# A decoder step: the multiply of LayerNorm's affine part moves from VectorE to GpSimd

## The reference, cut to what matters

```
x = layer_norm(ALPHA * x + gate * f(x), g, b)

def layer_norm(x, g, b):
    mu = mean(x); var = mean((x - mu)**2)
    return (x - mu) * rsqrt(var + 1e-5) * g + b
```

## Time and profile before

| | us |
|---|---|
| timed runs | 2422.81 median of 3 (2417.99 to 2425.23) |
| profiled execution, its own time | 2418.94 |
| its span, first to last instruction | 2417.2 |
| VectorE busy | 915.0 (38%), 1456 instructions |
| GpSimd busy | 388.4 (16%), 279 instructions |
| TensorE busy | 1675.2 (69%) |

### The profile page before, as it was taken

One profiled execution on the slowest core, in us unless ns is written; L12 is line 12 of the kernel. 1 busy time (PEld: TensorE's weight loads), 2 busy tenths in 40 slices (PEclk: granted clock), 3 DMA queues, 4 the chain that ended last, 5 costly groups with the idle time before them and its releaser, 6 DMA issues. The chain is left out here.

```text
span 2417.2 us, 21915 instructions
## 1 busy us (share of the span) xinstructions
PE 1675.2 (69%) x6774; PEld 695.2 (29%) x6775; DVE 915.0 (38%) x1456; ACT 387.5 (16%) x748; POOL 388.4 (16%) x279
## 2 busy tenths in 40 slices
PE   4565999487648999808977255555664739998980
PEld 1113444333323333304433122222221323333330
DVE  0112011547430000162020999999974450000006
ACT  0000011301112112221011111111111111221222
POOL 0000000000100000040020555555530100000004
PEclk8886999768759999958989566777777959999995
DMA  8884211142259989824220678778773066999973
GB/s 337 346 307 152 70 35 35 70 149 90 70 227 424 399 359 424 340 98 132 71 105 33 229 287 287 287 291 293 293 265 139 2 244 253 374 425 428 428 338 110
DMA packets 116715, 558.69 MB, mean 231 GB/s; under 512 B 13206, under 2 KB 22167, under 8 KB 101796
## 3 DMA queue, kind: packets, MB, share of 16 engines
q1 hardware_dynamic: 103000, 508.87, 54.3%
q0 software_dynamic: 7904, 28.45, 3.2%
q10 hardware_dynamic: 5740, 20.47, 2.1%
HBM read 517.62 MB, written 40.13 MB: 231 GB/s over the span
## 5 line engine op out<-in xcount | busy, mean ns | idle before, releaser
L1382 PE MATMUL ps<-arena_w,arena_r 128*64 128x512 f32 x1664 | 379.1, 612 | 31.3 <-issue 26.3
L1382 PEld LDWEIGHTS ps<-arena_w,arena_r 128*64 128x64 f32 x1664 | 126.9, 142 | 277.1 <-issue 270.9
L1364 PE MATMUL ps<-arena_w,arena_r 128*64 128x512 f32 x832 | 190.1, 605 | 19.2 <-ACT arena_r L1412 19.2
L1459 DVE TENSOR_TENSOR arena_r<-arena_r,ps 128x512 f32<-128x512 f32 x38 | 26.1, 688 | 439.9 <-ACT arena_r L1429 439.9
L1924 PE MATMUL ps<-arena_w,arena_r 128*32 128x512 f32 x504 | 146.0, 814 | 29.2 <-DMA arena_w<-in_cache_v_dram 29.2
L1878 POOL TENSOR_TENSOR xt<-arena_w,xt 128x1024 f32<-128x1024 f32 x48 | 121.1, 2523 | 161.7 <-DVE arena_w L2092 80.4
L352 PE MATMUL ps<-ident,arena_r 128*128 128x128 f32 (+1 forms) x200 | 41.8, 372 | 141.7 <-DVE arena_r L343 141.7
L151 PE MATMUL ps<-arena_w,arena_r 128*32 128x512 f32 x448 | 74.1, 823 | 58.2 <-DMA arena_w<-in_w_ada_dram 51.1
L1579 PE MATMUL ps<-arena_w,xt 128*128 128x512 f32 x256 | 111.8, 597 | 0.0
L441 PE MATMUL ps<-arena_w,xt 128*128 128x512 f32 x256 | 111.7, 597 | 0.0
L916 PE MATMUL ps<-arena_w,xt 128*128 128x512 f32 x256 | 111.1, 593 | 0.0
(11 more groups left out here) (315 smaller groups left out, 2282.7 us busy)
## 6 DMA issues: line engine op xcount, KB each, us to landing
arena_w<-in_w_exp_gate_dram SPq DMA_DIRECT2D x38, 2048.0 KB, 13.8
arena_w<-in_w_exp_up_dram SPq DMA_DIRECT2D x38, 2048.0 KB, 19.0
arena_w<-in_w_exp_down_dram SPq DMA_DIRECT2D x38, 2048.0 KB, 18.2
arena_w<-in_cache_v_dram SPq DMA_DIRECT2D x126, 512.0 KB, 5.2
arena_w<-in_w_ada_dram SPq DMA_DIRECT2D x12, 4096.0 KB, 13.4
arena_w<-in_cache_k_dram SPq DMA_DIRECT2D x96, 512.0 KB, 5.4
y_rows<-arena_r ACTq DMA_DIRECT2D x38, 512.0 KB, 10.7
lnr<-in_cache_k_dram SPq DMA_DIRECT2D x32, 512.0 KB, 5.8
```

Of the source, the lines that this page charges most:

```text
L1364: last = nc.tensor.matmul(psy[c][at:at + 64, :], ht[u][:, k, 64 * (1 - a):64 * (2 - a)], wd[u][:, k, c * 512:(c + 1) * 512], start=(k == 0 ...
L1382: last = nc.tensor.matmul(ps[at:at + 64, :], xgt[u][:, k, 64 * a:64 * (a + 1)], w[u][:, k, :], start=(k == 0), stop=(k == KT - 1), tile_po ...
```

## The change

`shift` is gone, with its five calls per stage. `offset`, which GpSimd runs, waits for `scaled` instead, does the product, signals `gained`, waits for that, and does the sum. The order of GpSimd's list is otherwise the same.

```diff
@@ stage_mix_output, VectorE
                 ln.mixed(v, i, r, [m.ps[b] for b in banks]).then_inc(ev, 1)
                 ln.stats(v, i, r)
-                if n:
-                    ln.shift(v, *order[n - 1])
-            ln.shift(v, *order[-1])
@@ LayerNorm
-    def shift(self, v, i, r):
-
-        nc, m = self.nc, self.m
-        self.scales += 1
-        v.wait_ge(self.scaled, self.scales)
-        nc.vector.tensor_tensor(m.x[0:r, i, :], m.x[0:r, i, :], m.lnr[0:r, 0, :], ALU.mult).then_inc(self.gained, 1)
-
     def offset(self, g, i, r):
         nc, m = self.nc, self.m
         self.offsets += 1
+        g.wait_ge(self.scaled, self.offsets)
+        nc.gpsimd.tensor_tensor(m.x[0:r, i, :], m.x[0:r, i, :], m.lnr[0:r, 0, :], ALU.mult).then_inc(self.gained, 1)
         g.wait_ge(self.gained, self.offsets)
         nc.gpsimd.tensor_tensor(m.x[0:r, i, :], m.x[0:r, i, :], m.lnr[0:r, 1, :], ALU.add).then_inc(self.done, 1)
@@ stage_combine, VectorE
                 ln.mixed(v, i, r, [y1[:, 0:512], y1[:, 512:1024]]).then_inc(f_ok, 1)
                 ln.stats(v, i, r)
-                if i:
-                    ln.shift(v, *TILES[i - 1])
-            ln.shift(v, *TILES[-1])
```

More of the change, by code:

```diff
@@ L944, in __init__ @@
         self.gained, self.done = sem("gained"), sem("done")
-        self.tiles = self.sds = self.scales = self.offsets = 0
+        self.tiles = self.sds = self.offsets = 0
     def mixed(self, v, i, r, halves):
```

## The result

| | before | changed |
|---|---|---|
| timed runs, median (lowest to highest) | 2422.25 us (2414.95 to 2426.34), 13 runs | 2430.87 us (2424.8 to 2436.11), 13 runs |
| ratio to before, 95% interval | | 1.0038 [1.0025, 1.005] |
| span of the profiled execution | 2417.2 us | 2429.1 us |
| combine stages, first gather's sum (L1496) to last add | 47.83, 47.83 us | 53.72, 53.70 us |
| output projections, last L952 to the next stage's L340 | 12.42, 12.41 us | 11.47, 11.46 us |

The ratio is +6 to +12 us, about a value of 9. The stages give 5.89 + 5.87 - 2 x 0.95 = +9.9 us. The two profiled spans differ by 11.9; the remaining 2 us lie in stretches in which both kernels run the same instructions, and such stretches vary from profile to profile.

The account below looks back on a forecast made before the run. VectorE's own sequence was taken to bound the combine stages, TensorE the output projections. Two combine stages at +6.5 us (+13.0) and projections at -1.9 gave +11.1 us, forecast 2432 us from a 2421.2 mean, range 2420 to 2438.

Parts of the forecast that it names:

- multiply 0: Combine stage: GpSimd's first multiply, behind tile 3's gathers, makes tile 2's weighted sum L1496 wait, +2.2 us.
- multiply 1: Combine stage: GpSimd's second multiply, behind tile 4's gathers, delays VectorE the same way again, +2.2 us.
- multiply 2 and add 2: Combine stage, tile 3: the multiply goes between the two L952, the add between the second and L960, +4.2 us.
- tile 4 to its last L971: Combine stage: multiply 3 and add 3 precede the second L952 and L960, 4.2 where one add cost 2.0, +2.2 us.
- behind it: Combine stage's end after the last L971: 6.3 us instead of 7.2, -0.9 us.
- end of a projection: After an output projection's last scaling: 4.8 us instead of 5.8, -0.94 us each, -1.9 for two.
- Strict turns: VectorE and GpSimd alternate whole instructions when both ask: combine stages +6.5 us each, total +11.1 us, chance 0.5.
- mirror case: VectorE's two L952 overlap in issue while GpSimd waits; no row showed who goes next, hence the wide bound.
- signs named beforehand: Combine stages: second L952 of tiles 3 and 4 near 2.8 us, L960 near 3.2, L1496 or L971 2.2 late.
- Rival 1: VectorE's two L952 count as one turn: combine stage +2.3 us, total +2.7, 2424 us; chance 0.3.
- rival 2: Combine stages: multiplies 0 to 3 fall beside VectorE's single-input work or waits, costing nothing; total -10.5 us, 2411; chance 0.08.
- Rival 3: Single-input VectorE work waits too: combine stage +7.3 us, total +12.7, 2434 us; chance 0.12 including worse interleavings.

Follow-up runs that it names:

- e3: Changed kernel with the combine stages' gate product as one 1024-column VectorE instruction instead of two of 512; ratio to before 1.0012, stages 49.07 and 49.08 us.
- e7: Kernel before with the combine stages' gate product as one 1024-column VectorE instruction instead of two of 512; single execution, stages 47.48 and 47.48 us.
- e2: Kernel before with the multiply moved to GpSimd in the two combine stages only; ratio 1.0052, 2433.48 us, stages 53.71 and 53.71 us.
- e4: Changed kernel with GpSimd's multiply over columns 0 to 511 only, so its result differs; ratio to before 0.9981, stages 48.33 and 48.30 us.
- e5: Kernel before with LayerNorm's multiply and add both on VectorE in the combine stages, GpSimd only gathering there; ratio 0.9958, 2412.85 us.
- e1: Kernel before with the multiply moved to GpSimd in the two output projections only; ratio 0.9988, projections' ends 11.46 us.
- e6: Changed kernel with normalisation and affine part joined in two VectorE instructions in all four stages, ScalarE's scaling and GpSimd's work gone; ratio to before 0.9889, 2395.43 us.

## Why the prediction was right

The forecast was slower, +11.1 us within -1 and +17 of the four executions' mean; measured are +6 to +12, and +9.9 by stages. The steps, second combine stage, forecast against the distances between successive L1488 (L1496) of the two traces:

| step | forecast | measured |
|---|---|---|
| tile 2's weighted sum: multiply 0 ahead, L979 gone | +2.2 - 1.14 = +1.06 | 14.64 - 13.72 = +0.92 |
| tile 2 to 3: multiply 1 ahead, L979 gone | +1.06 | 10.21 - 9.40 = +0.81 |
| tile 3 to 4: multiply 2 and add 2 in between, L979 gone | +4.2 - 1.14 = +3.06 | 12.37 - 9.41 = +2.96 |
| tile 4 to its last L971 | +2.2 | 10.25 - 8.11 = +2.14 |
| behind it | -0.9 | 6.23 - 7.19 = -0.96 |
| stage | +6.5 | +5.87 |
| end of a projection | -0.94 | -0.95 |

- **Strict turns** was the choice that decided between +11.1 and +2.7, and it was made from a single row in which GpSimd had to give way in spite of its queue; at 0.5 against 0.3, that it came out was in part luck. The mirror case holds: in the trace of after, the pair L949 at 5.42 us has a GpSimd instruction between its halves, and the signs named beforehand are there (second half 2.82 us, forecast 2.8; L957 3.19, forecast 3.2). e3 shows it by taking the place away, e7 that the place alone costs little. Rival 1's order is what e3's kernel does (forecast +2.3 per stage for it, measured +1.24, or +1.59 without the 0.35 of overhead saved), but it is not what the changed kernel does. One thing stays open: whether the engines alternate or whoever asked first goes. At the places read here the two come to the same, for the engine that went had also asked first: the multiply at 2401.47, the second half of L949 only at 2401.98.
- **The terms that were mis-sized** are the first two, by 0.14 and 0.25 us: the whole 2.2 us was charged, but the multiply starts before VectorE asks. Multiply 1 is issued at 2395.73, L968 only at 2396.01. That multiply ran for 0.28 us beside work that does not wait, and so far rival 2 was right; 0.28 of 2.35 us, where it needed all. That is 0.8 of the 1.2 us by which two stages were over-forecast.
- **Rival 3**, that one-input work waits too, is refuted for LayerNorm's instructions by L966 at 0.16 beside L975 and by e3's statistics at 1.29 beside L979. It is not refuted in general, and the prediction named only L2092 against it. In the attention stage of the kernel before, a one-input `TENSOR_SCALAR` waits in full: it ends at 1342.07, 0.03 us behind the GpSimd multiply (timeline). All 24 that were issued beside such a multiply do so; on its own it takes 0.17. A `COPY` (L2140) that met one took 1.60 us instead of 0.19. What sets these apart from a reciprocal, a reduction or the statistics, no run here shows.

```profile
1339.71 2.34 POOL L1878 TENSOR_TENSOR xt<-arena_w,xt 128x1024 f32<-128x1024 f32 x1
1339.83 2.24 DVE L2074 TENSOR_SCALAR small<-small 128x2 f32<-128x2 f32 x1
```

- **That L971 would wait though it handles a single column** came as forecast: 2.20 and 2.10 us.
- **The projections** came to 0.01 us. One detail was wrong and cost nothing: I had the sample tile's add stand ahead of the first full tile's L960; in the trace the sum went first (1.30 us at 584.86) and the add, issued at 585.15, waited for it (3.21 us).
- **The gathers** stayed hidden: the last tile's first instruction, L1488 at 2410.40, has no wait on them.

Why VectorE's 1.14 us per tile did not shorten the path is thus shown and not argued: e2 puts the loss in the combine stages, e3 takes away a place to cut in, e4 halves GpSimd's instruction and gets back the matching part, e5 takes GpSimd's arithmetic out and is faster than before with more work on the path.

## What to carry to other kernels

In these runs an elementwise instruction moved from VectorE to GpSimd was not off VectorE's path when both engines' instructions had two inputs in SBUF: it took its turn there, at twice the length (2.34 against 1.22 us), ahead of whatever came next, be that one column wide. Count the places where GpSimd can get in (each VectorE instruction with two SBUF inputs was one, and cutting one in two made another) against what it has in wait; while the queue had more, each place cost VectorE one whole instruction. Some instructions with one input wait as well. The move did pay at the end of a projection (0.95 us), where VectorE has nothing else to do and its own multiply took 3.33 us with the wait behind the add. Only the profile shows this gain; the timed runs of e1 cannot tell it. Where VectorE is the path, see first whether the two operations join one that it does already (e6).

## What the runs showed of the hardware that was not expected

- GpSimd can come between the halves of a pair of which VectorE issues the second before the first has ended (by 0.08 us in tile 3): 5.42 us for a pair that takes 1.29.
- A wait at a turn does not delay what has its input in PSUM: L949 in the first projection was issued at 583.48, in the middle of a multiply (582.73 to 585.08), and took 1.29 us for its pair.
- A 128x512 multiply on GpSimd takes 1.27 us and a 128x1024 one 2.35: from these two widths its cost is in proportion to the columns, with 0.2 us on top.
